# A two-block transformer kernel in float32: POOL's subtractions in pieces, q's weights ahead of the rope tables, and another place for the attention values

## The reference

```
first block, 2 layers l:
    h = rms_norm(x, attn_norm_g[l]);  proj = h @ w_in[l]            # 1024 -> 3584
    ret = retention_bidir(rq, rk, rv, decays);  ret = rms_norm(ret) * silu(rg)
    da  = diff_attention(norm(dq), norm(dk), dv, lam, slopes);  da = rms_norm(da) * (1 - lam_init)
    x = x + concat(ret, da) @ w_out[l]
    h = rms_norm(x, ffn_norm_g[l])
    x = x + (silu(h @ w_gate[l]) * (h @ w_up[l])) @ w_down[l]       # d_ff 2816
second block, 2 layers i, on x and ctx, with shift, scale and gate from
    mod = silu(c) @ w_mod[i] + b_mod[i]  (and the same for c_ctx)
    i = 0: neighbourhood attention over an 8 x 64 grid plus all context keys; ctx attends to itself
    i = 1: q, k with rope; sliding window |i-j| <= 128 plus context keys, sink logits
           (16 heads of q, 4 of k and v); only x is updated
    x = x + gate * (attention @ w_o)
    u = h @ w_up (1024 -> 2 x 2816); depthwise convolution over 3 positions, + bias
    x = x + gate * (a * silu(g)) @ w_down
```

## Time and profile before

| | |
|---|---|
| median of three runs | 3073.2 us |
| profiled execution, its own time | 3069.21 us |
| its span, first to last instruction | 3067.4 us |
| PE, PE weight loads busy | 97%, 78% |
| DVE, ACT, POOL busy | 52%, 37%, 34% |
| mean granted PE clock | 0.989 |
| HBM traffic | 88 GB/s over the span |

### The profile page before, as it was taken

One profiled execution on the slowest core, in us unless ns is written; L12 is line 12 of the kernel. 1 busy time (PEld: TensorE's weight loads), 2 busy tenths in 40 slices (PEclk: granted clock), 3 DMA queues, 4 the chain that ended last, 5 costly groups with the idle time before them and its releaser, 6 DMA issues.

```text
span 3067.4 us, 46468 instructions
## 1 busy us (share of the span) xinstructions
PE 2981.4 (97%) x16904; PEld 2398.4 (78%) x16904; DVE 1585.0 (52%) x2527; ACT 1144.6 (37%) x1735; POOL 1053.2 (34%) x458
## 2 busy tenths in 40 slices
PE   8999999999999999999999999999999899999999
PEld 6866788887857788877886687888888777878887
DVE  5357654556357544554315746541553348566372
ACT  4264441223274442232226733321332227543232
POOL 3433444443433444442220023332223240244443
PEclk9999999999999999999999999999999899999999
DMA  4421343433411344431111111121111110122222
GB/s 165 142 102 38 127 151 124 147 132 104 164 60 56 125 146 131 146 124 49 48 65 42 53 42 55 62 69 56 67 64 66 56 62 8 38 86 95 91 97 101
DMA packets 78029, 272.75 MB, mean 89 GB/s; under 512 B 8160, under 2 KB 15328, under 8 KB 77792
## 3 DMA queue, kind: packets, MB, share of 16 engines
q1 hardware_dynamic: 76256, 267.09, 26.2%
q10 hardware_dynamic: 1664, 4.18, 0.4%
HBM read 269.14 MB, written 2.10 MB: 88 GB/s over the span
## 4 chain that ended last, share of the span: by engine, by line
PE 58%; issue 26%; POOL 8%; DVE 5%; ACT 2%; POOLq 0%; DMA 0%; ACTq 0%; DVEq 0%
PE ps L663 43%; POOL w_lo L556 7%; PE ps L701 4%; PE ps L1085 1%; PE ps L772 1%; PE ps L1067 1%; PE ps L814 1%; DVE s_s L2081 1%; PE ps L928 1%; PE ps L917 1%; DVE s_s L2071 1%; PE ps L952 1%; PE ps L909 1%; DVE h_lo L1701 1%; PE ps L827 1%
## 5 line engine op out<-in xcount | busy, mean ns | idle before, releaser
L556 POOL TENSOR_TENSOR w_lo<-w_raw,w_hi 128x1024 fp32r<-128x1024 f32 (+1 forms) x364 | 945.0, 2596 | 1533.6 <-ACT w_hi L1178 1533.6
L663 PE MATMUL ps<-h_hi,w_hi 128*128 128x512 f32 (+1 forms) x2816 | 953.2, 372 | 8.2 <-POOL w_lo L556 4.2
L663 PE MATMUL ps<-h_hi,w_lo 128*128 128x512 f32 (+1 forms) x2816 | 945.1, 369 | 0.0
L663 PE MATMUL ps<-h_lo,w_hi 128*128 128x512 f32 (+1 forms) x2816 | 944.1, 368 | 0.0
L1178 ACT ACTIVATE w_hi<-w_raw 128x1024 fp32r<-128x1024 f32 (+1 forms) x364 | 406.4, 1116 | 1352.0 <-PE ps L663 1229.4
L663 PEld LDWEIGHTS ps<-h_hi,w_hi 128*128 128x128 f32 x2816 | 489.4, 188 | 116.2 <-issue 12.9
L663 PEld LDWEIGHTS ps<-h_hi,w_lo 128*128 128x128 f32 x2816 | 489.1, 188 | 90.8
L663 PEld LDWEIGHTS ps<-h_lo,w_hi 128*128 128x128 f32 x2816 | 488.4, 188 | 89.4 <-issue 0.7
L1855 DVE TENSOR_SCALAR conv_y<-u_pad,small 128x770 f32<-128x770 f32 (+1 forms) x88 | 176.3, 2004 | 192.2 <-ACT u_pad L1371 192.0
L1808 DVE SCALAR_TENSOR_TENSOR xT<-ps,mod,xT 128x512 f32 (+1 forms) x72 | 45.4, 659 | 306.7 <-PE ps L663 259.9
L1634 DVE CUSTOM_DVE_ANT_0 mod_junk<-mod_w,silu_c 128x1024 f32<-128x1024 f32 x96 | 139.3, 1451 | 123.5 <-DMA mod_w<-w_mod_dram 121.6
(11 more groups left out here) (213 smaller groups left out, 3708.4 us busy)
## 6 DMA issues: line engine op xcount, KB each, us to landing
mod_w<-w_mod_dram SPq DMA_DIRECT2D x96, 512.0 KB, 3.5
w_raw<-w_gu_dram SPq DMA_DIRECT2D x88, 512.0 KB, 3.4
w_raw<-w_down_dram SPq DMA_DIRECT2D x64, 704.0 KB, 4.1
w_raw<-w_up_dram SPq DMA_DIRECT2D x88, 512.0 KB, 3.4
w_raw<-w_in_dram SPq DMA_DIRECT2D x56, 512.0 KB, 3.5
w_raw<-na_qkv_dram SPq DMA_DIRECT2D x24, 512.0 KB, 3.4
w_raw<-w_out_dram SPq DMA_DIRECT2D x16, 512.0 KB, 3.5
n_bias<-rpb_dram SPq DMA_DIRECT2D x24, 256.0 KB, 3.1
```

The costliest lines, as they stand in the source:

```text
L556: pool.tensor_tensor(w_lo[par][:, 0:cols], w_raw[par][:, 0:cols], w_hi[par][:, 0:cols].bitcast(F32), ALU.subtract).then_inc(w_lo_ready, 1)
L663: last = pe.matmul(acc[par][:, to:to + n], w[par][:, k * P:k * P + P], r[:, k, frm:frm + n], start=begin, stop=end)
```

## The change

1. POOL makes `w_lo` with four subtractions of a quarter of the columns, and signals after the last. Its low parts of activations (`lo_tiles`) go in pieces of 256 columns.
2. SP issues the weights of q's first two pairs before the rope tables and the band, and waits for the norm only behind them. The casts of k's head norm move from the sixth tile of q's first unit to the third tile of its second.
3. In both attentions of block 2 PE's order is score s, values of s-4, turning of s-2.
4. ACT's first pair of each `glu` stage stands outside the loop.

```
+PIECES = 4
@@ SP, over ahead(phases)
                 if roped(ph):
+                    weights(dict(ph, pairs=(0, 2)))
                     sp.wait_ge(n_xn_ready, KT * ph["norm0"])
                     sp.dma_start(s_cos[:], d["rope"][0]).then_inc(tab["rope"], 16)
                     sp.dma_start(s_sin[:], d["rope"][1]).then_inc(tab["rope"], 16)
                     sp.dma_start(s_band[:], d["band"]).then_inc(tab["swa"], 16)
                 if "weight" in ph:
-                    weights(ph)
+                    weights(dict(ph, pairs=(2, 4)) if roped(ph) else ph)
@@ POOL, split
-                        pool.tensor_tensor(w_lo[par][:, 0:cols], w_raw[par][:, 0:cols],
-                                           w_hi[par][:, 0:cols].bitcast(F32), ALU.subtract).then_inc(w_lo_ready, 1)
+                        for frm in range(0, cols, cols // PIECES):
+                            piece = slice(frm, frm + cols // PIECES)
+                            last = pool.tensor_tensor(w_lo[par][:, piece], w_raw[par][:, piece],
+                                                      w_hi[par][:, piece].bitcast(F32), ALU.subtract)
+                        last.then_inc(w_lo_ready, 1)
@@ POOL, lo_tiles
-                    pool.tensor_tensor(h_lo[:, k, 0:T], source(k), h_hi[:, k, 0:T].bitcast(F32), ALU.subtract
-                                       ).then_inc(h_pool, 1)
+                    for frm in range(0, T, 2 * P):
+                        last = pool.tensor_tensor(h_lo[:, k, frm:frm + 2 * P], source(k)[:, frm:frm + 2 * P],
+                                                  h_hi[:, k, frm:frm + 2 * P].bitcast(F32), ALU.subtract)
+                    last.then_inc(h_pool, 1)
@@ PE, normed_units
-                    unit(ph, 0, 1, first)
+                    unit(ph, 0, 1, first, ends[0])
                 def tail(k):
...
-                    if k == 5:
+                    if k == (KT + 2 if ph["T"] == T2 and n == 2 else 5):
                         head_casts(ph, n // 2 - 1)
@@ PE, na (swa the same, with 32)
-                for s in range(48 + 3):
+                for s in range(48 + 4):
...
+                    if s >= 4:
+                        values(s - 4)
                     if 2 <= s < 50:
                         turn(s - 2)
-                    if s >= 3:
-                        values(s - 3)
@@ ACT, glu
-                units_of(ph, body)
+                units_of(ph, body, peel=1)
```

More of the change, by code:

```diff
@@ L1132, in values @@
                                 last.then_inc(s_values, 1)
-                for s in range(32 + 3):
+                for s in range(32 + 4):
                     if 0 < s < 32:
```

## The result

The changed kernel takes 3132.6 us (median of 4 runs, 3131.8 to 3135.4) where the kernel before, measured beside it, takes 3070.3: ratio 1.0204, 95% interval 1.0187 to 1.0222. It is 2% slower; I had said 3125. The profiled execution took 3132.4 us, with a span of 3130.6.

A forecast was written before the change was run, and what follows sets the result against it. PE was taken as the bound, busy 2981.4 of 3067.4 us. Terms 61.9 (pieces) - 0.6 - 8.7 - 5.2 + 6.4 = +53.8 on 3069.2 gave 3123.0; the forecast said 3125, range 3066 to 3143.

The forecast's parts named there:

- The step that decided: Gate and up stages of block 1: three waiting DVE operations get between POOL's four pieces; PE stands 1.37 us a pass, +53.6.
- the discount: Gate and up: the first of two stages has 0.6 us more slack, so two passes count 0.77 us instead of 1.37.
- Rival 1: Gate and up: piece 2 is asked for before `b_lo`, two DVE operations get in, 0.25 us a pass; 3079 to 3083; chance 0.15.
- rival 2: POOL's pieces follow so closely that nothing gets in; they cost only 0.4 us, held by slack; 3067 us; chance 0.13.
- `w_out`: Block 1's output projection: both products get in, last piece 1.0 us late in two passes of two layers, +4.0 (0 to 6).
- Down: Down stages: slack holds the two products, but the second pair's `w_lo` makes PE wait 0.4 us more six times, +2.3.
- `w_in`: Input projection behind its head-normed units: no loss expected from the pieces, 0.
- the last layer's convolution: Convolution stage: scale-and-add and two multiply-adds use up POOL's 1.5 us of slack; 0 to 0.28 us in 22 passes, +2.
- ACT's unrolled pair: First half gate stages: no table load in the loop, two waits of 0.3 us go, -0.6; avoids 20 x 0.2 = +4.
- q: q's first units: early weights -3.6, low clock that goes with the idle time -2.7, later casts -2.4; sum -8.7.
- Sliding window: Sliding window attention: DVE's tile copy stands ahead of `bias`, 1.0 us in six steps plus 0.4 at the tail, +6.4.
- Neighbourhood: Neighbourhood attention: the score comes earlier and feeds DVE earlier, so 14 steady waits go, -5.2 (0 to -6).

The follow-up runs named there:

- products_wait: The changed kernel with one more wait: in the gate and up stages VectorE starts the two modulation products only when `w_lo` is complete; 3075.5 us, ratio 1.0018.
- two-piece kernel: The changed kernel with `w_lo` in two pieces instead of four; 3058.3 us, ratio 0.9962 to the kernel before.
- pieces_only: The kernel before with only the two splits (`w_lo` in four pieces, `h_lo` in pieces of 256 columns); 3141.8 us, ratio 1.0239.
- whole_casts_early: The changed kernel with `w_lo` and `h_lo` whole again and the casts of k's sums back at step 5 of q's first unit; 3061.0 us, ratio 0.9968.

## Why the prediction was right

**The step that decided held.** Three operations get in, as the order of requests said. I put 1.37 us on a pass, measured 1.42 (12.30 less 10.88), and 53.6 us on the four stages, measured 57.5, which is 40 passes at the full price: the discount that I gave to the first pass of two stages is not seen. `w_lo` lasts 5.26 us where I had 5.33. Four pieces by themselves take 2.83 us (2.79). Rival 1 (two get in) and rival 2 (none) are excluded by the timeline, and products_wait shows what rival 2 would have brought.

**The Trainium skill** (SBUF — State Buffer, "Who interferes with whom") says that the one that issues first has the shared pair for its whole instruction and the other fully blocks. The traces agree with the blocking: in the two-piece kernel `b_lo`, and then the product, stood still behind POOL. Had the hold had its full length, the pass would have cost 2.0 us; it cost 1.42. In the pass shown, `b_lo` (0.69 us alone) ends 0.57 us behind the end of the first piece, and the second piece (0.74 us alone) 0.60 behind the end of `b_lo`: the hand changes 0.12 and 0.14 us before an instruction's end.

**Terms that were too small.** `w_out` +7.9 for 4.0: three passes of a layer wait, not two, PE for 0.66, 0.80 and 0.80 us and some 0.3 for each new start; 1.6 us of the 7.9 is a stretch of 3.4 us at half clock in layer 0, which the kernel before doesn't have there. Down +8.6 for 2.3: the second pair's wait grew by 0.43, as said, but each stage also waits at its entry, for the first unit's pieces (0.60 to 0.93 us), and there I had looked only at the steady slack. `w_in` +3.2 for 0, again in a stage's first passes. In the last layer's convolution the +1.4 is near my +2 but not from where I took it: no steady pass waits, the first of the two stages waits once, 0.50 us, at its entry. Timelines of PE in the changed kernel: block 1's output projection, the entry of a down stage, the input projection:

```profile
310.42 0.49 PE L672 MATMUL ps<-h_hi,w_hi 128*128 128x512 f32 x1 [0.80 <-POOL w_lo L562]
...
479.77 0.50 PE L710 MATMUL ps<-b_hi,w_hi 128*128 128x512 f32 x1 [0.60 <-POOL w_lo L562]
...
88.50 0.49 PE L672 MATMUL ps<-h_hi,w_hi 128*128 128x512 f32 x1 [0.36 <-POOL w_lo L562]
```

**ACT's unrolled pair.** Its two waits of 0.3 us went as said, and without the pieces it is worth 0.8 us a stage; with them nothing of that is left, and its protection (20 x 0.2 us) was not needed: pieces_only has the same loss without it.

**q** came out at 8.3 for 8.7, but the division was partly wrong: I gave the low clock to the early weights alone, since after the 2.01 us of idle time in the earlier trace rows the clock had not fallen. In whole_casts_early, where only that wait is left (1.99 us), it fell, and it did in pieces_only, behind the same 1.99 us.

**The attentions.** Sliding window +7.6 for +6.4: the copy's place, shown by taking it away. Neighbourhood -10.8 for -5.2: the order brings 8.4 us, the waits 4.5 of them; the step that failed is "PE does the same score and the same values either way", which priced the matmuls alone and not the changes between their kinds and the new starts (3.9 us). The kernel before also had 3.4 us at half clock here, worth 1.6 us. And here a gap pays: at the start of the attention POOL makes `w_lo` of the next stage's first unit, VectorE's scaling of the probabilities took 2.58 us behind the whole instruction and takes 0.95 between two pieces, and PE's wait for it is 1.25 us instead of 2.24.

**The sum.** Between the profiled executions the kernel grew by 63.2 us for my 53.8. The terms of the pieces, with the unrolled pair, came to 15.7 us more than I had (77.0 for 61.3, the half clock in `w_out` left out), most of it at the entries of the stages, where all errors have one sign. The neighbourhood attention gave 5.6 us more than I had, q and the sliding window together came out 1.6 worse, and the rest, half clock for the most part, took off 2.3. So it is in part luck that the total is nearer than its terms.

## What to carry to other kernels

Splitting a long instruction of one engine to let another in is paid by the owner: first count which operations of the other engine stand ready at each gap, then compare the sum of their durations with the slack of the split result. If only one of them is urgent, hold the others back with a wait, or make one gap and not three. That takes away the loss; that a gap gains anything is shown here in one place only, 1.0 us at the start of the neighbourhood attention. Look at the first passes of each stage as well as the steady one, since slack is smallest there.

## What the runs showed that I had not expected

A wait of 1.99 us before a stretch of PE work was followed by half clock when the one before it had been removed, and likewise 2.78 us with the other removed; removing either of two waits gives back less than half of what removing both gives (3.1 and 3.8 of 8.4 us). A wait of that size is not always followed by it: in the kernel before the clock stayed up behind 2.01 us.

Matmul order has a price with no idle time in it: 3.9 us in 48 steps of the neighbourhood attention, 2.0 of them from 21 changes between kinds of matmul that cost 0.09 us more each in the old order.
